# Gated linear attention: forget gates and queries projected with the weights stationary and the tokens moving

## The reference

```
f = cols[..., w:2 * w].astype(jnp.float32)
log_f = jnp.logaddexp(jnp.log(lb), jnp.log1p(-lb) + jax.nn.log_sigmoid(f))
k = (1.0 - lb) * jax.nn.sigmoid(-f)
...
G = jnp.cumsum(to_c(log_f), axis=3)                      # in chunks of 64 tokens
o_inter = jnp.einsum('bhtk,bhkv->bhtv', qt * jnp.exp(Gt), state)
attn = jnp.einsum('bhtk,bhsk,bhtsk->bhts', qt, kt, decay)
```

## Time and profile before

| | us |
|---|---|
| median of 3 runs | 2066.82 |
| lowest, highest | 2064.64, 2067.5 |
| span of the profiled execution | 2065.0 |

### The profile page before, as it was taken

How to read it: one execution, slowest core, us unless ns; L and a number is a source line. 1 busy time by engine, 2 the same in 40 slices (tenths; PEclk the granted TensorE clock), 3 DMA queues, 4 the chain that set the end, 5 groups by cost and what they waited for, 6 DMA issues and landing times.

```text
span 2065.0 us, 27987 instructions
## 1 busy us (share of the span) xinstructions
PE 1975.9 (96%) x10551; PEld 1682.8 (81%) x10551; DVE 1170.5 (57%) x2306; ACT 1031.2 (50%) x1700; POOL 308.9 (15%) x418
## 2 busy tenths in 40 slices
PE   7999999999999999899999999999999989999998
PEld 7977767777777777689999999999788777877887
DVE  3345378553899999753454344444443536736772
ACT  4654433344687887663544444445343555345341
POOL 0611122010000010302211122012010001401310
PEclk9999999999999999999999999999999999999999
DMA  4411222136699999522222222223243411121231
GB/s 148 139 52 41 62 63 68 34 95 254 238 358 367 339 365 355 206 61 85 69 70 73 72 65 75 70 72 91 74 152 124 137 46 62 41 62 62 62 102 41
DMA packets 178017, 255.58 MB, mean 124 GB/s; under 512 B 13565, under 2 KB 92234, under 8 KB 177882
## 3 DMA queue, kind: packets, MB, share of 16 engines
q1 hardware_dynamic: 168832, 221.33, 33.2%
q0 software_dynamic: 8784, 31.92, 4.1%
q10 hardware_dynamic: 266, 0.52, 0.1%
HBM read 239.57 MB, written 14.16 MB: 123 GB/s over the span
## 4 chain that ended last, share of the span: by engine, by line
PE 77%; DVE 11%; ACT 5%; DMA 4%; issue 2%; POOL 1%; SPq 0%; ACTq 0%; DVEq 0%
PE pb L2392 50%; PE pb L2420 5%; PE pb L2764 5%; DVE wlo L1561 3%; PE pb L2787 3%; PE pb L2988 2%; ACT whi L947 2%; PE pb L2907 2%; PE pb L2476 2%; PE pb L2489 2%; PE pb L2896 2%; DMA wraw<-w_up 1%; DMA wraw<-w_down 1%; PE pb L2653 1%; DVE arena L2166 1%
## 5 line engine op out<-in xcount | busy, mean ns | idle before, releaser
L1561 DVE TENSOR_TENSOR wlo<-wraw,whi 128x1024 fp32r<-128x1024 f32 (+4 forms) x430 | 491.8, 1154 | 518.8 <-ACT whi L947 514.3
L2392 PE MATMUL pb<-whi,AT_hi 128*128 128x512 f32 (+4 forms) x1992 | 768.5, 386 | 12.6 <-DVE arena L2166 5.3
L2392 PE MATMUL pb<-whi,AT_lo 128*128 128x512 f32 (+4 forms) x1992 | 727.5, 365 | 0.0
L2392 PE MATMUL pb<-wlo,AT_hi 128*128 128x512 f32 (+4 forms) x1992 | 725.6, 364 | 0.0
L947 ACT ACTIVATE whi<-wraw 128x1024 fp32r<-128x1024 f32 (+4 forms) x446 | 440.6, 993 | 384.4 <-PE pb L2392 318.2
L2392 PEld LDWEIGHTS pb<-whi,AT_hi 128*128 128x128 f32 x1992 | 376.6, 189 | 84.3 <-issue 39.2
L2392 PEld LDWEIGHTS pb<-whi,AT_lo 128*128 128x128 f32 x1992 | 375.7, 189 | 45.4
L2392 PEld LDWEIGHTS pb<-wlo,AT_hi 128*128 128x128 f32 x1992 | 377.1, 189 | 38.0 <-issue 2.6
L2420 PE MATMUL pb<-arena 128*128 128x128 f32 (+1 forms) x1180 | 176.9, 277 | 31.1 <-ACT arena L983 6.2
L2420 PEld LDWEIGHTS pb<-arena 128*128 128x128 f32 (+1 forms) x1180 | 143.6, 144 | 66.6 <-issue 11.4
L2764 PE MATMUL pb<-whi,AT_hi 128*128 128x512 f32 x256 | 103.9, 406 | 0.7 <-DVE AT_lo L1907 0.7
(11 more groups left out here) (312 smaller groups left out, 2357.0 us busy)
## 6 DMA issues: line engine op xcount, KB each, us to landing
wraw<-w_in_a SPq DMA_DIRECT2D x288, 128.0 KB
wraw<-w_gate SPq DMA_DIRECT2D x128, 256.0 KB
wraw<-w_up SPq DMA_DIRECT2D x128, 256.0 KB
wraw<-w_down SPq DMA_DIRECT2D x58, 512.0 KB
wraw<-w_in_b SPq DMA_DIRECT2D x40, 512.0 KB
wraw<-w_in SPq DMA_DIRECT2D x28, 512.0 KB
wraw<-w_mem_kv SPq DMA_DIRECT2D x16, 512.0 KB
wraw<-w_in_a SPq DMA_DIRECT2D x16, 512.0 KB
```

What stands on the lines that cost most here:

```text
L1561: dve.tensor_tensor(w_slot(wlo, p, p % SPL), raw_slot(p), w_slot(whi, p, p % SPL).bitcast(F32), ALU.subtract).then_inc(lo_done[p % SPL], 1)
L2392: mm = pe.matmul(ACC[bank][:, 0:n], a, b, start=kc == 0 and q == 0, stop=i == c["count"] - 1 and kk == per - 1 and q == 2)
```

## The change

`chunk` gets a mark `flip`, set for the forget gates and queries. `project_tile` then takes a 128-column tile of the weight piece (`whi`, `wlo`) as the stationary operand and all 512 tokens of `AT_hi` or `AT_lo` as the moving one, so that bank `ACC[t]` holds 128 features as rows and 512 tokens. Each chunk keeps its 96 matmuls. The 64 transposes of the two halves are gone, and so are ACT's copies into `l_tok`; the sigmoids and the copies into `lq` read the projection banks. Four places move with it: on DVE the splits of `vl`'s four pieces stand ahead of the scans, between them, behind the small tables and behind the first exponents; the arithmetic on the sigmoids waits bank by bank; PE's wait for `gl_od` goes into the loop; both score buffers are cleared at the start. On ACT in half 1, the squares stand ahead of the copies into `lq`.

```diff
-                chunk(f"{nm}l{hh}", [w_b[:, :, c:c + 512]], 512, 0, 8, 2)
+                chunk(f"{nm}l{hh}", [w_b[:, :, c:c + 512]], 512, 0, 8, 2, flip=nm != "v")
...
@@ POOL
-            pool.memset(lAs[0], 0.0).then_inc(S("lA_zero"), 1)
+            for a in lAs:
+                pool.memset(a, 0.0).then_inc(S("lA_zero"), 1)
             for hh in range(2):
-                wait_tp_read(pool, f"ql{hh}", 4)
-                pool.memset(lA, 0.0).then_inc(S("lA_zero"), 1)
...
@@ ACT
+                j = CH[f"fl{hh}"]
                 if hh:
-                    act.wait_ge(S("gl_o"), 4)
-                evac(f"fl{hh}", lambda t: l_tok[:, t, :], fed=hh == 0)
-                if hh == 0:
-                    after(CH["fl0"])
-                else:
+                    during(j)
                     act.wait_ge(S("gated1"), NT)
                 for i in range(4):
...
+                    wait_acc(act, j, i)
+                    act.activation(lf[:, i, :], ACC[i], ACT.Sigmoid)
+                    act.activation(lk[:, i, :], ACC[i], ACT.Sigmoid, scale=-1.0).then_inc(acc_free[i], 1)
+                after(j)
...
-                evac(f"ql{hh}", lambda t: l_tok[:, t, :])
-                act.wait_ge(S("gl_L"), 4 * hh + 4)
+                j = CH[f"ql{hh}"]
+                during(j)
                 if hh:
+                    act.wait_ge(S("gl_L"), 8)
                     squares(0)
                 for i in range(4):
-                    tcopy(f"ql{hh}", i, lq[:, i, :], tb(f"ql{hh}", i))
+                    wait_acc(act, j, i)
+                    act.activation(lq[:, i, :], ACC[i], ACT.Copy).then_inc(acc_free[i], 1)
+                after(j)
...
@@ DVE
-                wait_tp_read(dve, f"fl{hh}", 4)
                 for i in range(4):
                     H = 4 * hh + i
+                    wait_read(dve, f"fl{hh}", i)
...
+                query_piece = chunks[CH[f"ql{hh}"]]["first"]
+                feed(query_piece + SPL)
                 for h in range(4):
...
+                    if h == 1:
+                        feed(query_piece + 1 + SPL)
...
-                flow(f"ql{hh}")
+                feed(query_piece + 2 + SPL)
...
                     exponents(n)
+                feed(query_piece + 3 + SPL)
...
@@ PE
+                    if c["flip"]:
+                        ah, al = (w[:, p % SPL, kk * n + t * P:kk * n + t * P + P] for w in (whi, wlo))
+                        bh, bl = (a[:, (c["at"] + kc) % 12, :] for a in (AT_hi, AT_lo))
...
-                if hh:
-                    pe.wait_ge(S("gl_od"), 4)
...
-                for nm, following in (("f", "q"), ("q", "v")):
-                    project_piece(f"{following}l{hh}", 0)
-                    read_all(f"{nm}l{hh}")
-                    for i in range(4):
-                        transposes(f"{nm}l{hh}", i, [l_tok[:, t, P * i:P * i + P] for t in range(NT)])
-                    for i in (1, 2, 3) if nm == "f" else ():
-                        project_piece(f"ql{hh}", i)
+                project(f"ql{hh}")
+                project_piece(f"vl{hh}", 0)
```

More of the change, by code:

```diff
@@ L191, in build, with chunk @@
         CH = {}
-        def chunk(name, srcs, n, at, k, per, nt=NT, mem=False, order=None, bank=0):
+        def chunk(name, srcs, n, at, k, per, nt=NT, mem=False, order=None, bank=0, flip=False):
             first = len(pieces)
@@ L204, in chunk @@
             CH[name] = len(chunks)
-            chunks.append(dict(first=first, count=k // per, n=n, at=at, per=per, nt=nt, mem=mem, bank=bank))
+            chunks.append(dict(first=first, count=k // per, n=n, at=at, per=per, nt=nt, mem=mem, bank=bank, flip=flip))
         def tiled(w):
@@ L343, in build @@
         mem_units(1)
-        for hh in range(2):
-            tpu(f"fl{hh}", 4)
-            tpu(f"ql{hh}", 4)
         for c in range(3):
@@ L585, in build @@
         top[0] = l2_0
-        at_ltok = top[0]
-        l_tok = take(2048, NT, 512)
-        lA = l_tok.rearrange("p a b -> p (a b)").rearrange("p (s t) -> p s t", s=NT)
+        lA1_at = top[0]
+        lA1 = take(2048, NT, T)
         at_lq = top[0]
@@ L607, in build @@
         assert lA_at + 2048 <= gla_at
-        lAs = [view(lA_at, 2048, NT, T), lA]
-        diags = [view(at, 2560, NT, 640)[:, :, 0:P] for at in (lA_at, at_ltok)]
+        lAs = [view(lA_at, 2048, NT, T), lA1]
+        diags = [view(at, 2560, NT, 640)[:, :, 0:P] for at in (lA_at, lA1_at)]
         def halves(a, half):
@@ L916, in _ @@
             end_phase(pool, "POOL")
[L919 removed]
+            for a in lAs:
+                pool.memset(a, 0.0).then_inc(S("lA_zero"), 1)
             for hh in range(2):
[L921 to L922 removed]
                 for n in range(36 * hh, 36 * hh + 36):
                     half = 1 << n % 9
+                    if n % 9 == 0:
+                        wait_read(pool, f"ql{hh}", n // 9 % 4)
                     e2, q2 = halves(kq[n % 5], half)[1], halves(lq[:, n // 9 % 4, :], half)[1]
@@ L2322, in _ @@
                     if n % 9 == 0:
-                        dve.wait_ge(S("lA_zero"), hh + 1 + H % 2)
+                        dve.wait_ge(S("lA_zero"), 1 + H % 2)
                         if H >= 2:
@@ L2968, in _ @@
                         if i == 0:
+                            wait_read(pe, f"ql{hh}", h)
                             k, q = lk[:, h, :], lq[:, h, :]
@@ L2994, in _ @@
                                 project_tile(name, q, t)
+                        if H == 4 and i == 2:
+                            pe.wait_ge(S("gl_od"), 4)
                         if H == 4 and i in (2, 3):
@@ L3002, in _ @@
                     pe.wait_ge(S("gl_c"), 10 * H + 10)
+                    if H == 0:
+                        wait_tp_read(pe, "mat1", 8)
                     if H >= 2:
```

5 lines of the change are left out of this document (removed).

## The result

The changed kernel takes 2056.85 us (median of 4 runs, 2055.72 to 2057.51) against 2067.16 beside it (4 runs, 2064.64 to 2070.0). The ratio is 0.9946 with a 95% interval of 0.9934 to 0.9959, so it is faster by about half a per cent. The forecast was 2053.3 in a range of 2049.0 to 2059.5. Timed twice more, beside the kernel before each time, it took 2055.02 against 2068.99 (0.9942, 0.9926 to 0.9958) and 2054.30 against 2068.41 (0.9931, 0.9913 to 0.9950).

A forecast was written before the change was run, and what follows sets the result against it. PE, holding 77% of the chain, was taken as the bound, with gains from earlier loop starts: 6.9 + 6.6 = 13.5 us off the 2065.0 span gives 2051.5, plus 1.8 for the runs' median, 2053.3; range 2049 to 2059.5.

The forecast's parts named there:

- Half 0, 6.9: Half 0's prologue: its first score block with exponentials comes 6.9 us earlier, 35.2 after the stage's first matmul instead of 42.1.
- small wait for bank 0: Half 0: PE, done with fl0, waits 0.4 us for the sigmoids to free the first projection bank before ql0.
- wait of 1.2: Half 0: PE's 1.2 us wait for vl0's first split disappears; DVE's new order was said to decide this.
- Half 1, 6.6: Half 1: its loop starts 6.6 us earlier, after a clock fall takes 0.9 from a 7.5 gain.
- new wait of 2.6: Half 1: PE idles 2.6 us before vl1 until ACT's first query copy, behind the squares, frees bank 0; clock fall assumed.
- old fall lost 1.4: Half 1 of the kernel before: the halved clock made 96 matmuls take 23.39 us instead of 22.0, 1.4 lost.
- rival 1: Half 1: the clock stays up over PE's new wait, gain 14.4 us, time 2052.4; chance 0.25.
- 2 (the second prologue gives back more): Half 1's ACT and DVE chain is some 5 us longer than counted, gaining only 2: 2059; chance 0.14.
- 3 (the loops absorb): What follows the prologues absorbs the gain through DVE and POOL waits; under 4 us arrives, 2063 to 2067; chance 0.05.
- 4 (flipped matmuls slower): The 384 swapped projection matmuls stream slower; break-even 35 ns each, 2130 at plain fp32 pace; chance 0.04.
- 5: The transposes do not go; excluded because ql0's second piece directly follows its first; no chance given.

The follow-up runs named there:

- Transposes back: Changed kernel with 32 unread PE transposes per half put back, in two groups of 16, without their ACT copies: 2056.64 us, ratio 0.9941.
- Order: Changed kernel with DVE's splits of the value pieces back behind the scans, as in the kernel before; flip kept: 2053.82 us, ratio 0.9929.
- copies first: Changed kernel with ACT's query copies, and the high part behind them, ahead of the squares in half 1: 2053.18 us, ratio 0.9933.
- fill: Changed kernel with ten unread matmuls of 512 columns in PE's new wait in half 1: 2052.68 us, ratio 0.9925.
- late and order: Changed kernel with gate arithmetic ahead of the split of ql's last piece, and vl's splits back behind the scans: 2052.55 us, ratio 0.9924.
- late: Changed kernel with DVE doing arithmetic on each fl sigmoid as it comes, splitting ql's last piece afterwards: 2048.65 us (0.9909), again 2049.01 (0.9901).

## Why the prediction was right

**What bounds it.** Right: only the starts of the two loops moved. Loop 0 went from 84.7 to 84.4 and the rest from 183.5 to 183.3 (each with one fall in it; without a fall it is 181.9 before and 181.6 to 181.8 with the change). The forecast had them unchanged with half 1's first matmul 0.55 earlier within loop 0; it was 0.3 earlier.

**Half 0, 6.9.** Measured 6.9 (42.1 to 35.2), and every step in it within 0.2: arithmetic, logarithms, first scan, end of vl0's piece, high part, load, first exponential. The small wait for bank 0, taken at 0.4, is 0.4. Transposes back confirms that PE set this end: of the work put back, all but the wait of 0.6 came back. One reason in this step was wrong, though no number was. The prediction says that the new order on DVE decides whether vl0's first piece is split in time, and takes the wait of 1.2 off by it. Order puts the splits back behind the scans, and the wait is gone all the same. The first of them starts 23.4 after the stage's first matmul there (28.2 in the kernel before), and PE is through with ql0 only at about 25.4: it is the earlier sigmoids that make the split early enough.

**Half 1, 6.6.** Measured 5.9 in the prologue and 0.3 ahead of it, 6.2. Counted from the half's first matmul, the squares start 43.6 after it (forecast 43.75), vl1's piece 46.5 (46.6), the first exponential 56.2 (56.15), the first block 58.0 (57.9). The wait's cause, ACT's squares ahead of its copies, was shown by copies first and by order, both of which remove it.

**The clock.** That the new wait of 2.6 would bring a fall was right (three of three), and fill shows that the idle time brings it. It cost 1.1 where I had put 0.9. But the ground I gave for its price and its chance was thin, and in so far this term came out by luck. The prediction counts two falls behind three waits of 2.08 to 2.67, and takes the wait of 2.67 for one that does not bring a fall. In the third profile of the same kernel it brought one (PE's timeline, and a window behind it):

```profile
828.96 0.47 PE L2787 MATMUL pb<-whi,AT_hi 128*128 128x512 f32 x1 [2.67 <-DVE AT_lo L2005]
```
```profile
829.00:833.00 4.00, 4.00 (x11) 0.57 1.03 410
```

Over the fourteen profiles a fall came behind this wait of 2.67 in eleven, behind one of 2.29 near 1490 (which the prediction leaves out) in eight, behind the one of 2.15 in the last loop in eight, and behind one of 1.48 ahead of the stage in seven. The waits of 2.6 of order and of late and order, ahead of the first exponential block, were followed by a fall in the latter (1870) and not in the former, that of 3.3 of copies first was (1866), and the same wait of 2.08 in the kernel before brought one in two of four profiles. A wait of this length makes a fall likely, not certain. The sentence that the old fall lost 1.4 was wrong in its worth: 23.39 instead of 22.0 is what PE took, 0.1 is what the stage lost. It did no harm, since the forecast rebuilt half 1 step by step and did not add the 1.4 to a gain.
The rule of the Trainium skill (TensorE: Matmul & The Clock Gate, Part 4: PE-mode transpose), that transposes do not count as activity as matmuls do, would have had the old stretch with them fall more readily than the new one without; here the old one fell in two of four and the new one in three of three, and 32 transposes put back into half 1 brought no fall with them. So few profiles do not refute it, but rival 1, which rested on it and on the wait of 2.67, did not come.

**The sum.** 13.5 forecast for the stage; measured 376.5 to 363.2, that is 13.3, and with the other profiles 13.1 to 14.3 (the largest with a fall inside the kernel before's stage). With nothing else changed the span would be 2051.7, forecast 2051.5. In the first profile all else was 3.0 later when the stage began, of which 1.55 was there at fl0's first matmul (1647.88 against 1646.33) and the rest is the fall at 1662. Behind it eight score matmuls ahead of the stage took 3.65 instead of 1.96, after the same wait of 0.84. PE's timeline, before and then after:

```profile
1661.19 1.96 PE L2440 MATMUL pb<-arena 128*128 128x256 f32 x8 [0.84 <-ACT arena L983]
```
```profile
1662.72 3.65 PE L2445 MATMUL pb<-arena 128*128 128x256 f32 x8 [0.84 <-ACT arena L980]
```

In the changed kernel's second profile the stage began at 1686.6, 1.9 earlier than before. So the 3.5 us between the forecast and the first median is not in a term of the sum, it lies ahead of the stage, where executions of one kernel differ by more; the two other medians are 1.0 and 1.7 above the forecast. The three drops against the kernel beside it are 10.3, 14.0 and 14.1, mean 12.8.

**The rivals.** 1 (the clock stays up) did not come. 2 (the second prologue gives back more): counted from the half's first matmul it is 0.1 longer than forecast, not some 5, although its chain of changes between ACT and DVE was indeed without slack. Its price of 2059 is not its own sum: 6.9 and 2 off 2065.0, plus 1.8, make 2057.9. 3 (the loops absorb): no, they moved whole. 4 (flipped matmuls slower): 390 ns, nothing. 5: the order was what it said.

**Left open.** The mean start of the stage is 1687.8 in four profiles of the kernel before and 1690.0 in ten with the change, with single values from 1686.3 to 1695.3. Of these 2.2, 1.5 are there before fl0's first matmul (mean start 1645.5 and 1647.0), where no matmul is changed, and the other 0.7 is the fall between 1658 and 1666, 1.5 in five of ten. Whether such microseconds are regularly lost ahead of the stage or are chance, fourteen profiles cannot tell.

## What to carry to other kernels

When work is taken off the bounding engine, rebuild the chain behind it step by step to the next thing that is late; here the second half's end was set by DVE and ACT, and moving one split there (late) took another 4.5 us off the prologue, a third of what the change itself had brought in the stage, and the median was 5.3 lower than the changed kernel's beside it. A low clock seen on PE is not a loss until what waits behind it has been looked at: at full clock PE may only wait. Where an effect is some microseconds in 2000, compare the lengths of the stages in the profiles, which repeat to 0.1 where no fall lies in them, and not the spans, which carry every clock fall of the program.

## What the runs showed of the hardware

- The falls of TensorE's clock come in one execution of a kernel and not in the next, with the same waits ahead of them. In four profiles of the kernel before, the wait of 2.08 us was followed by one in two, the wait of 2.67 in two, the wait of 2.15 in three and the wait of 2.29 in two. A fall between 1686 and 1694 came in two of these four and in five of the ten with the change. Where PE is the bound each cost 0.8 to 1.7 us. The spread of one kernel's runs, 1.8 to 9.2 us, is of the size that a few falls more or less make; that it comes from them is argued, since only the profiled runs show their clock.
- In the one profile of fill, the fall behind an idle PE was bought off with unread matmuls: 10 of them took 2.2 of a wait of 2.6 and saved 1.1.
- Taking the weights or the activations as the stationary operand made no difference for matmuls of 128 x 128 against 128 x 512 in this type: 390 against 393 ns.
